# Other places in SBUF for the work tiles and the split tiles of a two-block transformer kernel

## The reference

```python
def first_block(x, mem, ...):
    for l in range(DEPTH):                                   # DEPTH = 2
        h = hybrid_mixer(x, pos, row, col, w_in[l], ...)
        x = layer_norm(ALPHA * x + h, ln1_g[l], ln1_b[l])
        h = memory_cross_attention(x, mem, x_wq[l], x_wkv[l], x_wo[l])
        x = layer_norm(ALPHA * x + h, ln2_g[l], ln2_b[l])
        h = conv_ffn(x, f_w_up[l], f_conv_k[l], f_conv_b[l], f_w_down[l])
        x = layer_norm(ALPHA * x + h, ln3_g[l], ln3_b[l])
    return x

def second_block(x, c, ...):
    c_act = jax.nn.silu(c)
    for layer in range(DEPTH):
        ...
        x = sandwich(x, c_act, mixer, ...)                   # even: SSD + differential attention
        x = sandwich(x, c_act, mlp, ...)                     # odd: retention + window attention
    return x
```

## Time and profile before

| | |
|---|---|
| median of 3 runs | 3782.71 us |
| profiled execution: time of the run | 3777.81 us |
| profiled execution: span | 3775.8 us |
| mean granted TensorE clock | 0.966 |
| TensorE matmul busy | 3556.0 us, 94% |
| GpSimd busy | 2070.7 us, 55% |
| VectorE busy | 1606.6 us, 43% |
| ScalarE busy | 1012.6 us, 27% |

### The profile page before, as it was taken

How to read it: one execution, slowest core, us unless ns; L and a number is a source line. 1 busy time by engine, 2 the same in 40 slices (tenths; PEclk the granted TensorE clock), 3 DMA queues, 4 the chain that set the end, 5 groups by cost and what they waited for, 6 DMA issues and landing times.

```text
span 3775.8 us, 44923 instructions
## 1 busy us (share of the span) xinstructions
PE 3556.0 (94%) x17537; PEld 2778.3 (74%) x17537; DVE 1606.6 (43%) x2437; ACT 1012.6 (27%) x1955; POOL 2070.7 (55%) x2134
## 2 busy tenths in 40 slices
PE   8999988999999999889998999998899989989998
PEld 6677776888776777768885666776788767668886
DVE  3564435655436553467554444323422143233222
ACT  2344224211223441332112453332211123212111
POOL 5444573767553446556774454443567643446664
PEclk9999999999999999999998999998899989989999
DMA  4222222665221213236542222212233322122332
GB/s 137 59 65 62 84 87 73 197 191 165 82 74 53 68 42 114 71 115 192 179 134 68 62 64 62 74 53 62 84 100 95 95 62 62 45 78 84 96 94 73
DMA packets 578761, 345.19 MB, mean 91 GB/s; under 512 B 15999, under 2 KB 562040, under 8 KB 578552
## 3 DMA queue, kind: packets, MB, share of 16 engines
q1 hardware_dynamic: 574605, 337.34, 30.6%
q10 hardware_dynamic: 3947, 4.99, 0.4%
HBM read 340.14 MB, written 2.14 MB: 91 GB/s over the span
## 4 chain that ended last, share of the span: by engine, by line
PE 85%; DVE 6%; ACT 5%; issue 2%; DMA 1%; POOL 1%; SPq 0%; ACTq 0%; DVEq 0%; POOLq 0%
PE gemm L220 23%; PE gemm L223 22%; PE gemm L226 22%; PE outs L300 6%; PE scores L300 6%; PE gemm L255 1%; PE scores L1450 1%; PE gemm L256 1%; PE gemm L257 1%; DMA w_raw<-in_w_in 1%; ACT tiles L633 1%; POOL w_low L201 1%; DVE work L1439 0%; DVE x_t L1105 0%; DVE tiles L1102 0%
## 5 line engine op out<-in xcount | busy, mean ns | idle before, releaser
L199 POOL CAST w_high<-w_raw 128x512 fp32r<-128x512 f32 (+1 forms) x1065 | 695.7, 653 | 1589.8 <-PE gemm L226 1206.9
L201 POOL TENSOR_TENSOR w_low<-w_raw,w_high 128x512 fp32r<-128x512 f32 (+1 forms) x1065 | 1386.4, 1302 | 85.3
L220 PE MATMUL gemm<-x_high,w_high 128*128 128x512 f32 x2584 | 720.6, 401 | 24.1 <-DVE tiles L1855 5.2
L223 PE MATMUL gemm<-x_low,w_high 128*128 128x512 f32 x2584 | 695.2, 391 | 0.0
L226 PE MATMUL gemm<-x_high,w_low 128*128 128x512 f32 x2584 | 692.0, 390 | 0.0
L220 PEld LDWEIGHTS gemm<-x_high,w_high 128*128 128x128 f32 x2584 | 478.9, 190 | 134.3 <-issue 17.1
L223 PEld LDWEIGHTS gemm<-x_low,w_high 128*128 128x128 f32 x2584 | 487.6, 189 | 105.2
L226 PEld LDWEIGHTS gemm<-x_high,w_low 128*128 128x128 f32 x2584 | 485.2, 188 | 102.8
L220 PE MATMUL gemm<-split_tiles,w_high 128*128 128x512 f32 (+1 forms) x1456 | 391.1, 389 | 7.4 <-DVE tiles L1540 2.6
L223 PE MATMUL gemm<-split_tiles,w_high 128*128 128x512 f32 (+1 forms) x1456 | 380.4, 382 | 0.0
L226 PE MATMUL gemm<-split_tiles,w_low 128*128 128x512 f32 (+1 forms) x1456 | 378.5, 381 | 0.0
(11 more groups left out here) (342 smaller groups left out, 3613.9 us busy)
## 6 DMA issues: line engine op xcount, KB each, us to landing
w_raw<-in_mlp_w SPq DMA_DIRECT2D x112, 512.0 KB, 4.0
w_raw<-in_mod_w SPq DMA_DIRECT2D x96, 512.0 KB, 3.8
w_raw<-in_w_in SPq DMA_DIRECT2D x88, 512.0 KB, 3.7
w_raw<-in_f_w_up SPq DMA_DIRECT2D x88, 512.0 KB, 5.0
w_raw<-in_e_w_in SPq DMA_DIRECT2D x48, 512.0 KB, 3.9
w_raw<-in_f_w_down SPq DMA_DIRECT2D x32, 512.0 KB, 4.2
w_raw<-in_o_w_in SPq DMA_DIRECT2D x30, 512.0 KB, 3.8
w_raw<-in_w_branch SPq DMA_DIRECT2D x48, 256.0 KB, 2.6
```

The source lines that it names most:

```text
L199: me.pool.tensor_copy(WH[:, h, 0:n], W32[:, s, c0:c0 + n]).then_inc(sem["w_rounded"], 1)
L201: me.pool.tensor_tensor(WL[:, h, 0:n], W32[:, s, c0:c0 + n], WH[:, h, 0:n].bitcast(F32), ALU.subtract).then_inc(sem["w_split"], 1)
L220: me.pe.matmul(o, WH[:, h, (k - k0) * cols:(k - k0 + 1) * cols], src(k)[0], start=begin and k == 0, stop=False)
L223: me.pe.matmul(o, WH[:, h, (k - k0) * cols:(k - k0 + 1) * cols], src(k)[1], start=False, stop=False)
```

## The change

Seven tensors change their place in the order of opening. `T2` is opened after the small tensors mask, diag, zero, params, second_params and stats; `R` and `RF` are opened last, after the two layer_params. No instruction is added, removed or moved: the lists of all five engines are the same row for row, and only the SBUF addresses in the operands differ.

```diff
@@ build @@
         T = sb("tiles", [P, TT, S])
         MAT = sb("mats", [P, len(CONSTS), P])
         M = {n: MAT[:, i, :] for i, n in enumerate(CONSTS)}
-        T2 = sb("work", [P, 8, S])
-        with nc.sbuf_tensor("split_tiles", [P, RT, S], F32R) as R:
-            pass
-        RF = sb("plain_tiles", [P, RT, S])
         mask = sb("mask", [P, 3 * P])
         diag = sb("diag", [P, P])
         zero = sb("zero", [P, 1])
         prm = sb("params", [P, 112])
         PB = sb("second_params", [P, 267])
         st = sb("stats", [P, 64])
+        T2 = sb("work", [P, 8, S])
         scale_rows = sb("scales", [P, P])
         MD = sb("modulations", [P, 96])
...
         layer_params = [sb(f"layer_params{l}", [P, 266]) for l in range(DEPTH)]
+        with nc.sbuf_tensor("split_tiles", [P, RT, S], F32R) as R:
+            pass
+        RF = sb("plain_tiles", [P, RT, S])
```

## The result

The changed kernel takes 3803.06 us (median of 6 runs, 3795.79 to 3808.95), the kernel before 3782.99 (median of 6, 3777.81 to 3783.96). The ratio is 1.0054, with a 95% interval of 1.0041 to 1.0067. Forecast were 3782.7 us and no change. The profiled execution has a span of 3800.4 us, 24.6 more than before; the profile before is that of the fastest of its six runs, so 24.6 is more than the 20.1 us between the medians.

What follows compares the result with a forecast made beforehand. TensorE's float32r matmuls were taken to bound the kernel. Four terms of 0 (split_tiles operand, VectorE and ScalarE, L1439, transfers) left the three-run median of 3782.7 us, no change at 0.78, with a range of 3770 to 3803.

Steps and rivals of the forecast that it cites:

- What bounds the kernel: TensorE, busy 94% of the span and 85% of the chain of waits; the pace of float32r matmuls counts.
- Moving operand in split_tiles: 4416 matmuls reading split_tiles at the new offset: cost 0, taken from plain float32 matmuls on scales, 111 against 112 ns.
- Where in such a block a tile starts makes no difference, as long as it is a multiple of 64: Blocks of 2,048 bytes: x_high at 128 and split_tiles at 1,664 both took about 227 ns a matmul.
- VectorE and ScalarE at 0: Their instructions on split_tiles or work cost nothing more; for L1439 at most 5 us on the path, taken as 0.
- Transfers at 0 to 0.6 us: Transfers landing in work at the new offset: value 0, likely upper end 0.6 us, 20.3 us kept for the range.
- The 0.3 us: Transfers into work: 69 beats a row instead of 68 by the page, 1.5% of 20.3 us; changed no term.
- Rival 1: L220, L223, L226 on split_tiles: one more 64-byte block a matmul, 7.1 ns, 27 to 31 us slower, 3812; chance 0.07.
- Rival 2: Transfers into work get slower, by up to 20.3 us, 3803; chance 0.05.
- rival 4: TensorE's clock: less time at half clock through small shifts, 13 us faster, 3770; chance 0.04.
- Rival 3: Matmuls on split_tiles: the new start hides 14 ns of start-up, 62 us faster at most, 3721; chance 0.04.
- The test written down: Matmul distance on split_tiles in the profile after: 227 ns confirms the forecast, 234 rival 1, 213 rival 3, x_high at 227.
- theory E: From the experiments, not the prediction: float32r matmul pace depends on moving start less stationary start, modulo 256; 226.7 ns at 0.

Runs made afterwards that it cites:

- The bursts: Kernels of float32r matmul bursts on TensorE alone, none of the reference's computation, operand starts varied: 226.7 ns with both starts at 128, 233.3 with the moving one at 160.
- the kernels at 192 and 448: split_tiles' start modulo 256 or 512: kernel before, work 32 bytes on, split_tiles 64, 3790.34 us; changed kernel, 32 unused bytes ahead of split_tiles, 3792.74 us.
- the weights moved: The changed kernel with w_high and w_low moved by 32 bytes, all other tensors keeping their starts modulo 512: 3835.39 us, 1.0137 of the kernel before.

## Why the prediction was wrong

**What bounds the kernel: right.** All but 1.6 us of the 24.6 is the distance between float32r matmuls.

**Moving operand in split_tiles: here it failed.** The step "I take 0, the value of the nearest row" took a plain float32 row for a float32r one. The prediction said that the row "doesn't close the question, because it reads half as fast", and took it all the same. The bursts show that plain float32 is blind to the start (429.1 and 429.2 ns), so its 111 against 112 ns were no evidence. The width hid it too: float32r of 128 columns takes 110.8 to 111.7 ns. The measured term is 6.0 ns on 4032 matmuls and -3.1 on 384, 23.0 us, where the sum had 0. That the time came out at the upper end of the range, 3803, says nothing for the prediction: that end was set by transfers, and those in the chain are longer by 1.8 us in all.

**"Where in such a block a tile starts makes no difference, as long as it is a multiple of 64": wrong.** x_high at 128 and split_tiles at 1,664 modulo 2,048 looked like two different places. They are the same place modulo 256, and the same as the weights'. 192 and 448 are multiples of 64 and take 229.1 ns. With 128 columns of weights the trace held no second difference to compare with. It did hold 24 float32r matmuls whose weights are 16 columns wide, so that they start every 64 bytes:

```profile
2072.56 2.03 PE L220 MATMUL gemm<-x_high,w_high 128*16 128x512 f32 x8 [2.60 <-DVE tiles L1855]
2074.42 2.02 PE L223 MATMUL gemm<-x_low,w_high 128*16 128x512 f32 x8
2076.28 2.02 PE L226 MATMUL gemm<-x_high,w_low 128*16 128x512 f32 x8
```

1.86 us / 8 = 232.5 ns from one to the next, on a moving operand that otherwise takes 227. Fewer weight columns alone bring it to 231.2 in the bursts (32 columns at difference 0), so these rows do not prove the cause, but they show that the distance is not fixed by the moving operand alone.

**VectorE and ScalarE at 0: right, as far as the traces tell.** L509 and L512 have their old times, and L1439's median moves with or without the offset. **Transfers at 0 to 0.6 us: right for the first two**; the third differs from run to run.

**The Trainium skill's page "SBUF — State Buffer", section "Door 1: The DMA port swizzle", with its lines of 16 bytes,** gave 0 as well, for a reason that did not bear on it. It speaks of consecutive accesses and the lines they cross. Measured here is that the starts of two streams, moving and stationary, matter by how they stand to each other: 226.7 against 233.3 ns, with every start a multiple of 16. The 0.3 us by the Trainium skill's page "DMA: Bandwidth & Descriptors", section "How a descriptor splits into AXI transactions", are shown by no run here.

**Rival 1** gave 3812 us and named the right place and nearly the right size (7.1 ns against 6.0 to 6.7). Its size was near by luck, since its reason, one more block of 64 bytes, is refuted by the kernels at 192 and 448, by the weights moved, and by the 256-column matmuls, which it would have made slower. It had 0.07, too little for the only moving operand at full pace whose new start no row covered. **Rival 2** (transfers) and **rival 4** (mean clock 0.968 after and 0.966 before, and single runs of the kernel before lie anywhere from 0.962 to 0.969) did not happen. **Rival 3** did not either: nothing brings the distance below 226.6 ns.

**The test written down** was right: "234 ns would be rival 1 ... both with x_high left at 227" is what the profile shows. It could not tell rival 1's reason from theory E's; the weights moved by 32 bytes could.

The cause that is shown: for float32r with 512 moving and 128 stationary columns, and starts on multiples of 32 bytes, the difference of the two starts modulo 256 sets the distance, alone on the core and in the kernel, from either side. That both reads meet at the same part of SBUF is an explanation that was only argued.

## What to carry to other kernels

Where float32r matmuls of 512 columns bound a kernel, give the moving and the stationary operands the same start modulo 256 bytes, on a multiple of 32 (at 144 and 144 the same start cost 233.3 ns); a small tensor opened between them can cost 6 ns in 227 on each. A tensor whose size is no multiple of 256 belongs behind them, or needs bytes to fill up. And a row counts as evidence for another form only if it has the same type and the same width: here the plain float32 row of 128 columns was blind to the very thing that was asked.

## What the runs showed that was not expected

The stationary operand's place changes the pace of the moving one, with no other engine at work: 226.7 ns at equal starts, 228.7 at 64 bytes ahead, 233.1 to 234.2 at the other multiples of 32, and up to 240.1 with the moving operand off the multiples of 16. The effect is small with 64 or 32 stationary columns: 228.3 to 231.7 ns at the three differences tried. Starts in step are not the best for every width: 256 columns take 119.6 ns at difference 0 and 114.2 with the moving operand at 64 and the stationary one at 128. Plain float32 matmuls had the same pace at both starts that were tried.
